# Differential attention: the rotary partner of a query or key tile made by a VectorE shuffle out of PSUM instead of a TensorE product

## The reference, cut to what matters

```python
def rope(x, pos):
    d = x.shape[-1]
    half = d // 2
    inv_freq = ROPE_THETA ** (-jnp.arange(half, dtype=F32) * (2.0 / d))
    ang = pos.astype(F32)[:, :, None] * inv_freq
    cos = jnp.cos(ang)[:, :, None, :]
    sin = jnp.sin(ang)[:, :, None, :]
    xf = x.astype(F32)
    x1, x2 = xf[..., :half], xf[..., half:]
    return jnp.concatenate([x1 * cos - x2 * sin, x2 * cos + x1 * sin], axis=-1).astype(x.dtype)

def diff_attention_group(q, k, v, pos, layer, lambdas, subln):
    ...
    q = rope(q.reshape(bsz, s, 2 * hh, d), pos).reshape(bsz, s, hh, 2, d)
    k = rope(k.reshape(bsz, s, 2 * hh, d), pos).reshape(bsz, s, hh, 2, d)
    ...
        p1 = masked_softmax(jnp.einsum('bqhd,bkhd->bhqk', q1b, k1, preferred_element_type=F32) * scale, mask)
        p2 = masked_softmax(jnp.einsum('bqhd,bkhd->bhqk', q2b, k2, preferred_element_type=F32) * scale, mask)
        return jnp.einsum('bhqk,bkhe->bqhe', p1 - lam * p2, vf)
```

## Time and profile before

| | us |
|---|---|
| median of 3 runs | 2877.63 |
| lowest, highest | 2875.4, 2879.02 |
| the profiled execution | 2880.98 |
| its span in the trace | 2879.1 |
| TensorE busy | 2794.0 |
| VectorE busy | 1388.3 |
| GpSimd busy | 1356.5 |
| ScalarE busy | 863.3 |

### The profile page before, as it was taken

One profiled execution on the slowest core, in us unless ns is written; L12 is line 12 of the kernel. 1 busy time (PEld: TensorE's weight loads), 2 busy tenths in 40 slices (PEclk: granted clock), 3 DMA queues, 4 the chain that ended last, 5 costly groups with the idle time before them and its releaser, 6 DMA issues.

```text
span 2879.1 us, 36730 instructions
## 1 busy us (share of the span) xinstructions
PE 2794.0 (97%) x14544; PEld 2169.2 (75%) x14544; DVE 1388.3 (48%) x2274; ACT 863.3 (30%) x1605; POOL 1356.5 (47%) x1106
## 2 busy tenths in 40 slices
PE   8999999999989999999999999999999998999997
PEld 5988777777878877677886666788787755788886
DVE  3412556666566123435847666524725956411113
ACT  3011332330130143322336354232223234222222
POOL 2445224224535654558765544844545413644443
PEclk8999999999999999999999999999999999999999
DMA  7111222232321221223321112222323321323322
GB/s 271 45 59 52 66 95 71 67 96 92 110 77 59 78 72 56 74 98 117 97 63 55 59 59 74 90 90 84 106 82 102 125 51 43 114 88 91 99 86 75
DMA packets 244836, 243.73 MB, mean 85 GB/s; under 512 B 5392, under 2 KB 234640, under 8 KB 244048
## 3 DMA queue, kind: packets, MB, share of 16 engines
q1 hardware_dynamic: 243376, 237.89, 26.0%
q0 software_dynamic: 1312, 3.80, 0.5%
HBM read 233.16 MB, written 7.34 MB: 84 GB/s over the span
## 4 chain that ended last, share of the span: by engine, by line
PE 84%; DVE 11%; ACT 2%; issue 2%; SPq 1%; POOL 0%; DMA 0%; DVEq 0%; ACTq 0%; POOLq 0%
PE psum L947 23%; PE psum L949 22%; PE psum L948 21%; PE psum L1210 4%; PE psum L1189 1%; PE psum L1145 1%; DVE columns L2668 1%; PE psum L1165 1%; PE psum L1478 1%; PE psum L1144 1%; PE psum L1327 1%; PE psum L1214 1%; PE psum L1498 1%; SPq L784 1%; PE psum L1098 0%
## 5 line engine op out<-in xcount | busy, mean ns | idle before, releaser
L947 PE MATMUL psum<-columns,columns 128*128 128x512 f32 (+1 forms) x3464 | 1345.8, 389 | 13.8 <-POOL columns L3393 4.9
L949 PE MATMUL psum<-columns,columns 128*128 128x512 f32 (+1 forms) x3464 | 1266.0, 365 | 0.0
L948 PE MATMUL psum<-columns,columns 128*128 128x512 f32 (+1 forms) x3464 | 1265.0, 365 | 0.0
L3393 POOL TENSOR_TENSOR columns<-columns,columns 128x512 fp32r<-128x512 f32 (+1 forms) x676 | 908.4, 1374 | 438.5 <-ACT columns L1872 405.3
L3389 POOL TENSOR_TENSOR columns<-columns,columns 128x512 fp32r<-128x512 f32 x392 | 423.6, 1111 | 975.9 <-PE psum L949 772.9
L947 PEld LDWEIGHTS psum<-columns,columns 128*128 128x128 f32 x3464 | 656.3, 189 | 197.3 <-issue 74.3
L948 PEld LDWEIGHTS psum<-columns,columns 128*128 128x128 f32 x3464 | 657.0, 190 | 123.8 <-issue 26.2
L949 PEld LDWEIGHTS psum<-columns,columns 128*128 128x128 f32 x3464 | 655.4, 189 | 113.2
L1872 ACT ACTIVATE columns<-columns 128x1024 fp32r<-128x1024 f32 (+2 forms) x154 | 136.8, 936 | 171.1 <-PE psum L949 166.1
L2668 DVE SCALAR_TENSOR_TENSOR columns<-columns,columns,columns 128x256 f32<-128x256 f32 x224 | 154.1, 742 | 0.0
L2650 DVE SCALAR_TENSOR_TENSOR columns<-columns,psum 128x512 f32<-128x512 f32 x80 | 54.7, 684 | 187.9 <-PE psum L1210 183.9
(11 more groups left out here) (418 smaller groups left out, 2730.4 us busy)
## 6 DMA issues: line engine op xcount, KB each, us to landing
columns<-in_w_merge SPq DMA_DIRECT2D x32, 1024.0 KB, 6.6
columns<-in_w_ada SPq DMA_DIRECT2D x24, 1024.0 KB, 5.5
columns<-in_w_in SPq DMA_DIRECT2D x22, 1024.0 KB, 5.4
columns<-in_ev_w_in SPq DMA_DIRECT2D x22, 1024.0 KB, 5.2
columns<-in_ffn_gate SPq DMA_DIRECT2D x22, 1024.0 KB, 5.3
columns<-in_ffn_up SPq DMA_DIRECT2D x22, 1024.0 KB, 5.3
columns<-in_ffn_down SPq DMA_DIRECT2D x16, 768.0 KB, 4.8
columns<-in_ffn_down SPq DMA_DIRECT2D x16, 640.0 KB, 4.4
```

The costliest lines, as they stand in the source:

```text
L947: mm(dst, weights(0, k), moving(0, k), start=start and k == 0, stop=False)
L948: mm(dst, weights(0, k), moving(1, k), start=False, stop=False)
L949: last = mm(dst, weights(1, k), moving(0, k), start=False, stop=stop and k == k_tiles - 1)
L3393: last = g.tensor_tensor(low[:, c], raw[:, c], high[:, c].bitcast(F32), ALU.subtract)
```

## The change

The host lays the 32 features of each half of a head's query and key columns in quarters of 16: first half's first 16, second half's first 16, first half's last 16, second half's last 16. A feature's partner is then 16 partitions away, inside the same group of 32 partitions. The frequencies and the signs follow this order (`sign16`, which another layer already uses). VectorE makes the partner tile with a shuffle within each group of 32 partitions, straight out of the PSUM tile into `raw2`. ScalarE's copy, the permutation product on TensorE and the two semaphores between them are gone, the sine product now has the scale 0.125 for queries, and both its inputs, like those of the addition, lie in SBUF.

```diff
@@ TensorE, ev_qk_out
-                def swap(n):
-                    pe.wait_ge(raw_ready, n + 1)
-                    if n:
-                        pe.wait_ge(roped, n)
-                    mm(psum[:, 2 * BANK:3 * BANK], c2("swap32"), raw2[:, n % 2, :], start=True, stop=True).then_inc(swapped, 1)
-
...
-                    if k == ROPE_AT and 1 <= n <= 16:
-                        swap(n - 1)
@@ ScalarE, ev_qk_out
-                    if k == 0 and 1 <= n <= 16:
-                        i = n - 1
-                        act.wait_ge(gemm_done, JOB0["ev_qk"] + i + 1)
-                        if i >= 2:
-                            act.wait_ge(roped, i - 1)
-                        f(raw2[:, i % 2, :], psum[:, i % 2 * BANK:(i % 2 + 1) * BANK], ACT.Copy, scale=0.125 if is_query(i) else 1.0).then_inc(raw_ready, 1)
@@ VectorE, ev_xbc
-                        order(v.scalar_tensor_tensor(out=halves(sind), in0=halves(sind), scalar=c2("sign32"), in1=r_tok, op0=ALU.mult, op1=ALU.mult))
+                        order(v.scalar_tensor_tensor(out=halves(sind), in0=halves(sind), scalar=c2("sign16"), in1=r_tok, op0=ALU.mult, op1=ALU.mult))
@@ VectorE, ev_qk_out
                 def cosines(n):
-                    dve.wait_ge(raw_ready, n + 1)
-                    order(v.scalar_tensor_tensor(out=qk2[:, qk_tile(n), :], in0=psum[:, n % 2 * BANK:(n % 2 + 1) * BANK],
+                    src = psum[:, n % 2 * BANK:(n % 2 + 1) * BANK]
+                    dve.wait_ge(gemm_done, JOB0["ev_qk"] + n + 1)
+                    order(v.stream_shuffle(raw2[:, n % 2, :], src, [p ^ 16 for p in range(32)]))
+                    order(v.scalar_tensor_tensor(out=qk2[:, qk_tile(n), :], in0=src,
                                                  scalar=0.125 if is_query(n) else 1.0, in1=cosd, op0=ALU.mult, op1=ALU.mult))
 
                 def rope(n):
-                    x, swp = qk2[:, qk_tile(n), :], psum[:, 2 * BANK:3 * BANK]
-                    dve.wait_ge(swapped, n + 1)
-                    order(v.tensor_tensor(swp, swp, sind, ALU.mult))
+                    x, swp = qk2[:, qk_tile(n), :], raw2[:, n % 2, :]
+                    order(v.scalar_tensor_tensor(out=swp, in0=swp, scalar=0.125 if is_query(n) else 1.0, in1=sind, op0=ALU.mult, op1=ALU.mult))
                     v.tensor_tensor(x, swp, x, ALU.add).then_inc(roped, 1)
                     dve.wait_ge(roped, n + 1)
@@ the host's layout
+def rotary_quarters(w):
+
+    w = np.asarray(w).copy()
+    heads = w[:, :, 2576:2576 + 2 * D].reshape(1, D, 32, 2, 2, 16)
+    w[:, :, 2576:2576 + 2 * D] = np.swapaxes(heads, 3, 4).reshape(1, D, 2 * D)
+    return w
```

More of the change, by code:

```diff
@@ L69 @@
 PACK2 = Pack([("ones", 128), ("ident", 128), ("norm_mix", 16), ("norm_ffn", 16), ("norm_final", 8),
-              ("inv_diff", 1), ("inv_mla", 1), ("sign32", 1), ("sign16", 1), ("half_pi", 1), ("sgn_c", 1),
+              ("inv_diff", 1), ("inv_mla", 1), ("sign16", 1), ("half_pi", 1), ("sgn_c", 1),
               ("conv_w", 48), ("conv_b", 12), ("d_skip", 8), ("gate_norm", 8), ("subln", 1), ("lambdas", 256),
-              ("swap32", 128), ("swap_mla", 128), ("rot_c", 128), ("tri", 128), ("sub_sums", 64), ("sel", 2048),
+              ("swap_mla", 128), ("rot_c", 128), ("tri", 128), ("sub_sums", 64), ("sel", 2048),
               ("dt_bias", 1), ("a_log", 1), ("reset", 512), ("s5_skip", 4), ("b_glu", 4), ("q_norm", 3), ("kv_norm", 2),
@@ L660, in build @@
         y_summed = sem("y_summed")
-        raw_ready = sem("raw_ready")
         roped = sem("roped")
-        swapped = sem("swapped")
         v_ready = sem("v_ready")
@@ L3577, in packed_keys_values @@
     return np.ascontiguousarray(np.concatenate([heads[..., 0:64].reshape(1, 256, SEQ), heads[..., 64:P].reshape(1, 256, SEQ)], axis=2))
+def rotary_quarters(w):
[3 more added lines that the diff above has]
+    return w
 def tables2(i):
     a, b = np.arange(P)[:, None], np.arange(P)[None, :]
-    s32, smla, rot = (np.zeros((P, P), np.float32) for _ in range(3))
-    for p in range(P):
-        s32[p ^ 32, p] = 1
+    smla, rot = (np.zeros((P, P), np.float32) for _ in range(2))
     for p in range(P):
@@ L3606, in tables2 @@
         "norm_mix": by_partition(i["norm_mix_2"], 8), "norm_ffn": by_partition(i["norm_ffn_2"], 8),
-        "norm_final": by_partition(i["norm_final_2"], 8), "inv_diff": np.tile(inv(32), 4), "inv_mla": inv_mla, "kr_first": first_rows, "kr_second": 1 - first_rows,
-        "sign32": np.tile(np.repeat([-1, 1], 32), 2).astype(np.float32), "sign16": sign16,
+        "norm_final": by_partition(i["norm_final_2"], 8), "inv_diff": np.tile(inv(32).reshape(2, 1, 16).repeat(2, 1).reshape(64), 2), "inv_mla": inv_mla, "kr_first": first_rows, "kr_second": 1 - first_rows,
+        "sign16": sign16,
         "half_pi": np.full(P, np.pi / 2, np.float32), "sgn_c": np.repeat([-1, 1], 64).astype(np.float32),
@@ L3613, in tables2 @@
         "lambdas": np.broadcast_to(g("ev_lambdas_2").reshape(1, 256), (P, 256)),
-        "swap32": s32, "swap_mla": smla, "rot_c": rot, "tri": np.where(b >= a, 0, NEG).astype(np.float32), "sel": sel, "sub_sums": sub_sums,
+        "swap_mla": smla, "rot_c": rot, "tri": np.where(b >= a, 0, NEG).astype(np.float32), "sel": sel, "sub_sums": sub_sums,
         "dt_bias": rows(g("ev_dt_bias_2")), "a_log": rows(g("ev_a_log_2")), "reset": reset,
@@ L3642, in layout @@
         "s5_bc": np.ascontiguousarray(np.stack([both(bre, bim), both(bim, bre), both(cre, cim), both(cim, cre)], 1)),
-        "ev_w_in": n["ev_w_in_2"], "ev_w_out": n["ev_w_out_2"], "od_w_in": replicated_rope_key(n["od_w_in_2"]), "w_glu": n["od_w_glu_2"],
+        "ev_w_in": rotary_quarters(n["ev_w_in_2"]), "ev_w_out": n["ev_w_out_2"], "od_w_in": replicated_rope_key(n["od_w_in_2"]), "w_glu": n["od_w_glu_2"],
         "w_uq": packed_queries(n["od_w_uq_2"]), "w_ukv": packed_keys_values(n["od_w_ukv_2"]), "od_w_out": n["od_w_out_2"],
```

## The result

The changed kernel is slower: 2886.95 us against 2876.48 us (medians of ten runs each), ratio 1.0035 with a 95% interval of 1.0027 to 1.0043. That is +10.1 us with 7.8 to 12.4, where I had forecast +6.2 and a range from -8 to +12. The profiled execution of the changed kernel has a span of 2889.7 us, 10.6 more than before; its 2891.58 us lie 4.6 above the median of its ten, as the profiled execution of before, with 2880.98 us, lies 4.5 above 2876.48.

What follows compares the result with a forecast made beforehand. TensorE, busy for 97% of the span, was taken as the bound, with VectorE late in places. Terms -0.86 + 5.6 - 4.3 + 2.6 + 2.0 - 0.86 + 0.4 + 1.6 gave +6.2 us, forecast 2884 us, range 2870 to 2890.

Steps and rivals of the forecast that it cites:

- The price of a swap: Each permutation product on TensorE, run as two matmuls, costs 0.86 us; removing all 16 brings at most 13.8 us.
- the swap ahead of stretch A: Swap 0, before the end of tile 1, is a plain gain: -0.86 us.
- stretch A: Tiles 1 to 4, VectorE already late: held rotations make TensorE wait, tile 5 starts at T+26.8 instead of 21.2, +5.6 us.
- The operations: VectorE per tile: shuffle 0.74 us; sine product and addition with two SBUF inputs 0.7 alone, about 1.7 beside GpSimd's subtraction.
- Stretch B: Tiles 5 to 13: even swaps gain 4.3 us; odd rotations, held by GpSimd, are waited for and lose 2.6 us.
- Stretch C: Rotation 13 grows from 1.4 to 3.4 us, delaying the reciprocal and the square roots at line 1519: +2.0 us.
- Stretch D: Tiles 14 to 16: swap 14 gives -0.86 us; VectorE is full at tile 15 and its rotation is waited for, +0.4.
- one such stretch: Clock: among the new waits, one 3.4 us stretch at half rate, after the 4.6 us wait: +1.6 us.
- the rival of the clock: Clock falls at each new wait from about 1.5 us: four more half-rate stretches, +6.8, 2891 us; chance 0.13 shared with shuffle.
- The kernel without collisions: Rival: two-SBUF operations don't collide with GpSimd, or the loss is hidden: -9.2, 2868 us; chance 0.12.

Runs made afterwards that it cites:

- partner in PSUM: The changed kernel, but the shuffle writes the partner tile into PSUM bank 2 instead of SBUF; 2873.26 us, ratio 0.9982 to the kernel before.
- sine product's result in PSUM: The changed kernel, but the sine product writes into PSUM bank 2, so the addition reads PSUM and SBUF; 2879.73 us, ratio 1.0007.
- before, with a shuffle: The kernel before plus an unused shuffle out of PSUM into SBUF ahead of each cosine product; 2878.55 us, ratio 1.0001.
- after, with a product: The changed kernel with an unused product of the swap's size put back on TensorE at the same places; 2890.93 us, ratio 1.0044.
- PSUM, at once: The changed kernel with the partner tile in PSUM and the rotation directly behind the cosine product (ROPE_AT 1 instead of 4); 2872.86 us, ratio 0.9976.
- SBUF, at once: The changed kernel, partner tile still in SBUF, with only the rotation moved directly behind the cosine product (ROPE_AT 1); 2885.63 us, ratio 1.0020.
- PSUM, at once, spread: The changed kernel with partner tile in PSUM, rotation directly behind the cosine product, and gate products one per tile; 2866.35 us, ratio 0.9957.
- before, spread: The kernel before with only the eight gate products spread, one per tile instead of one every other step; 2877.40 us, ratio 1.0000.
- after, spread: The changed kernel, partner tile in SBUF and rotation at step 4, with the gate products one per tile; 2883.28 us, ratio 1.0021.
- PSUM, spread: The changed kernel with partner tile in PSUM, rotation at step 4, and the gate products one per tile; 2871.40 us, ratio 0.9978.
- the run with the spread alone: The changed kernel, partner tile in SBUF, with nothing else altered but the gate products one per tile; 2883.28 us, ratio 1.0021.
- the first experiment: The changed kernel, but the shuffle writes the partner tile into PSUM bank 2 instead of SBUF; 2873.26 us, ratio 0.9982.

## Why the prediction was right

First an account of the stage in every profiled execution, from the start of GpSimd's first split in it (1575.63 us before, 1575.97 after) to the start of its last (1758.91, 1767.93). Taken off its length are all idle gaps of TensorE over 30 ns ("waits"), and half of the time at half rate that lies outside waits; that half is my estimate of what the clock cost.

| us | stage | waits | at half rate (in waits) | clock's cost | left over |
|---|---|---|---|---|---|
| before | 183.3 | 7.5 | 6.8 (0.2) | 3.3 | 172.5 |
| after | 192.0 | 24.3 | 23.9 (6.2) | 8.8 | 158.9 |
| partner in PSUM | 178.0 | 12.8 | 13.7 (0.8) | 6.4 | 158.8 |
| sine product's result in PSUM | 185.0 | 17.4 | 20.5 (3.1) | 8.7 | 158.9 |
| before, with a shuffle | 183.5 | 9.2 | 3.4 (0) | 1.7 | 172.7 |
| after, with a product | 193.9 | 13.7 | 17.1 (1.4) | 7.9 | 172.3 |
| PSUM, at once | 176.7 | 15.4 | 3.4 (0) | 1.7 | 159.6 |
| SBUF, at once | 191.1 | 23.5 | 13.7 (1.1) | 6.3 | 161.3 |
| PSUM, at once, spread | 170.9 | 9.9 | 3.4 (0) | 1.7 | 159.3 |
| before, spread | 183.3 | 7.5 | 6.8 (0) | 3.4 | 172.4 |
| after, spread | 188.4 | 20.0 | 23.9 (4.5) | 9.7 | 158.7 |
| PSUM, spread | 176.0 | 10.7 | 13.7 (1.2) | 6.2 | 159.1 |

What is left over is the same in all kernels with the products (172.3 to 172.7) and, except for one, in all without (158.7 to 159.6); what the 161.3 of the rotation at once with the partner in SBUF has in addition is not known. The step between is the price of the sixteen swaps, 13.6 us where I had said 13.8. For the change it reads: -13.6 for the swaps, +16.7 for waits, +5.5 for the clock, +8.7 together.

- **The price of a swap, 0.86 us, and of the swap ahead of stretch A.** The first split starts 0.5 us earlier in a stage that began 0.3 later: -0.9.
- **The operations.** Shuffle 0.73 (0.74 said). Sine product and addition 0.69 outside a split, 1.77 and 1.63 inside (1.7 said). The row of the first block in the earlier trace rows (1.78 and 1.66) carried over almost exactly; it is the same kind of operations against the same GpSimd pass. The prediction reads 1.66 as 0.69 plus about one GpSimd operation; the surplus is 0.9 to 1.1 us, where an operation of that pass takes 1.3 (5.34 for four).
- **Stretch A.** From the end of tile 1 (T = 1596.8 now), tiles 3, 4 and 5 start at 9.1, 15.7 and 26.0 us; said were 9.2, 16.2 and 26.8. The waits are 2.65, 0.8 and 4.0 against 2.8, 1.4 and 4.6. So the stretch cost 4.8 us, not 5.6; the difference is mostly rotation 2, whose addition got in ahead of GpSimd (0.69 us).
- **Stretch B.** The waits of odd tiles are 1.0 and three times 1.65; by the prediction's terms they were to be 1.1 and 1.7 each. From tile 8 to tile 13 the difference to before stands still, that is, two gained swaps (1.7 us) are paid by one wait of 1.65 us.
- **Stretch C.** 5.4 us wait where before it was 2.5: +2.9, and less swap 13's 0.86, +2.0, as said.
- **Stretch D.** The size came out, by another path. The prediction had rotation 15 waited for, and no addition is; TensorE waits 0.8 us for VectorE's weighing (at line 1480) and 2.4 for its copy of a head's output (at 1490), where before it waited 2.0 for the latter. That is +1.2, and less swap 15's 0.86, about the +0.4 said.
- **The clock is the term that was mis-sized.** The sum without it had +4.6; waits less swaps are +3.1 (24.0 less 7.1, less 13.8). The stage lost 8.7, so 5.6 us are left, and the clock's estimate, read independently from the granted clock, is 5.5. The step that failed was "one such stretch", +1.6 us. There were two new ones, at the waits of 4.0 and 2.4 us, of 6.8 us each, and the old one had grown from 3.4 to 6.8. That the total is no further off is in part luck: the waits were priced 1.5 us too high and the clock 3.9 too low, which partly cancels.
- **The rivals.** In the profile of the change the clock did not fall after the waits of 0.8 to 2.65 us in B and at tiles 3 and 4, but after those of 4.0, 5.4 and 2.4 us. That is less often than the rival of the clock had it, with longer stretches. In the run with the spread alone it did fall after a wait of 2.65 and one of 1.6 us, so this rival isn't refuted for every execution. The kernel without collisions was to take 2868; the first experiment, which is that kernel, took 2873. Swaps that bring nothing even there are real (waits at tiles 3 to 5 and at line 1511). In stretch A it lost 1.1 us, where the sum had -0.1. Its waits less the swaps are -8.3 us against before, near the -9.2 of that sum. The clock, which the sum had at nothing, took back 3.1.

How far this holds for the ten-run medians: the mean granted clock over the ten executions of the changed kernel is 0.9837, against 0.9866 to 0.9873 for the kernel before in the later batches. Within either kernel, executions with 0.001 less of it took 1.4 to 1.8 us longer, so this difference goes with some 4 to 7 of the 10.1 us. This is a correlation, and an estimate from it. Open: why the clock fell at one wait and not at another of the same length, and what the change costs at an unchanged clock; no run here controls it. The last 1.6 us of the profiled difference lie behind the stage. The granted clock differs there as well: over 2330 to 2460 us it is 0.88 after and 0.92 before.

## What to carry to other kernels

Taking a product from the busiest engine is worth its length only as far as the engine that takes over its work isn't the one waited for; list the waits at each place of the product first, not the shares of busy time. When an operation's inputs move from PSUM to SBUF, look at who else works in SBUF at that moment: beside GpSimd the same operation cost 0.9 to 1.1 us more here, and leaving the intermediate tile in PSUM turned a loss of 10 us into a gain of 5. Before moving an operation to where it has room, look at what is queued behind it. When waits change, look at the granted clock too, and count only the time at half rate in which the engine had work.

## What the runs showed of the hardware

- A shuffle works out of PSUM into PSUM: 0.691 us for 128x512 (0.733 into SBUF).
- A VectorE operation with two SBUF inputs of 128x512 takes 0.69 us alone and 1.63 to 1.77 us in a row against GpSimd's subtractions. A PSUM input frees it, a PSUM output doesn't.
- GpSimd pays as well: its four subtractions took 5.76 us beside rotation 7, against 5.34 at the same place before.
- TensorE's granted clock fell to 1.2 GHz for 6.8 us at waits of 4.0, 5.4 and 2.4 us, from 1.3 to 3.3 us before the wait's end, and stayed at 2.4 GHz at one of 2.65 us. In the run with the gate products spread, the same wait of 2.65 us was followed by 3.4 us at 1.2 GHz. A wait's length alone didn't tell.
